# First attention of a two-block fp32 model: forget rows earlier, the head groups' norm and turn earlier, modulation steps partly behind the attention

## The chip, the cores and the metric

The kernel runs on one core of one Trainium2 chip. The metric is the device time of one execution in microseconds. The unchanged kernel took 992.53 us, the median of three runs (992.22, 992.53 and 996.78).

## The reference

The input is one sequence of 256 tokens with 1024 channels in fp32. The first block is: RMS norm, one projection, eight heads of "forgetting" attention and eight heads of "stick-breaking" attention (head width 64), an RMS norm of each group of eight heads, an output projection, a gated feed-forward part with a causal convolution of three taps, and a final RMS norm. The second block has two layers whose norms are modulated by `mod = silu(c) @ w_ada + b_ada`, 6 x 1024 numbers a layer.

```python
F = cumsum(log_sigmoid(f_logit + forget_bias))                    # per head
logits = q.k/sqrt(64) + F[t] - F[s], s <= t; p = softmax(logits); o_fox = p @ v
A[t,s] = sigmoid(z[t,s]) * prod_{s<j<t}(1 - sigmoid(z[t,j])), s < t;  o_sb = A @ v
o = concat(rmsnorm(o_fox, fox_out_g), rmsnorm(o_sb, sb_out_g)); x = x + o @ w_out
h = rmsnorm(x, ffn_norm_g); u = causal_dwconv(h @ w_up); x = x + (silu(gate) * val) @ w_down
mod = silu(c) @ w_ada[i] + b_ada[i]     # two layers, 1024 x 6144 each, used from the second block on
```

## The kernel before

**Weights.** All weights pass through TensorE in chunks of 1 MB, numbered through the kernel: `IN1` 0 to 11 (projection), `OUT1` 12 to 15 (output), `UP1` 16 to 37, `DOWN1` 38 to 48, `QKV` 49 on. A chunk has two units (h = 0, 1), so unit number u = 2c + h. SyncE loads a chunk into one of four raw buffers, as soon as the low part of the chunk four before it has been made. ScalarE rounds a unit to its high part (`split_unit`, L504), VectorE subtracts to get its low part (L856), and TensorE multiplies with both. There are four buffers of high and low parts: ScalarE makes the high part of unit u when TensorE has finished unit u - 4 (`unit_done`). One unit is 24 matmuls (hi x hi, lo x hi, hi x lo).

**Order.** Every engine's program is written out by hand, and an engine does its instructions strictly in that order. In the first attention, all engines walk over slots (c, h), c from 0 to 13: TensorE multiplies unit (c, h), the other two prepare unit (c + 2, h), and tables (`SCORES1`, `EXPS1`, `PROBS1`, `VALUES1`) say in which slot each head's scores, exponentials, turns and value products come. Heads 0 to 7 are the forgetting group (g = 0), 8 to 15 the stick-breaking group (g = 1). `place(c)` on VectorE (L1140 to L1152) takes a projected chunk out of the PSUM bank to its place. The slots in `EARLY` do this ahead of the slot's split.

**Forget rows.** `forget` on ScalarE (L691, L693) and `nlf` on VectorE (L1249) give -log f; `forget_sums` on TensorE (L1697 to L1703) sums it up. VectorE copies the sums (`f_rows`, L1252), ScalarE issues two small DMAs that put them into spare rows of the keys (`forget_move`, L699), and TensorE's first scores (L1712) wait for these, for `f_cum`, and for the first two placed chunks.

**Group norms.** For g = 0: VectorE `fox_outputs` (L1203), ScalarE `output_squares` (L708), VectorE `output_mean` (L1220), ScalarE `output_rms` (L715, L717), VectorE `output_norm` (L1227 to L1232), TensorE `output_turn` (eight transposes, L1788), then ScalarE `output_hi` (L725) and VectorE `output_lo` (L1239). The same for g = 1, whose turned halves are the operand of the second half of the output projection (`out1_chunk(2, ...)` on); the first half, `out1_chunk(0 and 1, ...)`, uses g = 0.

**Modulation.** GpSimd pulls 1 MB pieces of `w_ada` (`fetch`, L458) into two buffers; VectorE adds each to an accumulator (`ada(n)`, L871). The pull for step n is issued when step n - 2 is done. Steps 0 to 7 sit in slots of the first attention (`ADA_AT1`), 8 to 13 in the pairs of `UP1` (`ADA_UP1`), 14 and 15 at the head of `DOWN1`, 16 to 23 in its loop. TensorE's `mod_sums(0)` (L1636) needs steps 0 to 7.

**After the output projection** VectorE's `add_up` splits units 32 and 33, and adds four PSUM banks to the residual (L943); ScalarE squares them (L509), TensorE sums the squares (L1521), then `mod_sums(0)`, and after the norm the first up-projection (L1452). In a pair of `UP1` VectorE splits four units (L856), does its `ada` if it has one, eight convolution steps (L965) and two steps for the hidden rows (L978, L981).

Of the kernel before, what the change touches and what calls it, by code (L numbers as in the profile page):

```python
# [8 lines left out]
ALU = mybir.AluOpType  # L9
# [47 lines left out]
PROBS2 = [(4, 0), (5, 0), (6, 0), (7, 0), (9, 0), (10, 0), (11, 1), (12, 1)]  # L57
VALUES2 = [(5, 0), (6, 0), (8, 0), (8, 1), (11, 0), (11, 1), (12, 1), (13, 1)]

ADA_AT1 = [(3, 0), (4, 0), (4, 1), (5, 0), (6, 0), (7, 0), (7, 1), (8, 0)]  # L60
ADA_UP1 = (1, 3, 4, 6, 8, 9)
ADA_AT2 = [(0, 0), (2, 0), (5, 0), (7, 0), (8, 0), (10, 0), (12, 0), (13, 0)]
LAST = 12
QK_AT, V_AT = (0, 1, 2, 3, 5, 6, 8, 9), (4, 7, 10, 11)
# [24 lines left out]
def model_kernel(nc, x, attn_norm_g, w_in, forget_bias, fox_out_g, sb_out_g, w_out, ffn_norm_g, w_up,  # L89
# [3 lines left out]
    with ctx:  # L93
# [396 lines left out]
        def _(act):  # L490
# [238 lines left out]
            for c in range(14):  # L729
                for h in range(2):  # L730
                    if (c, h) == (1, 0):
                        forget()
                    if (c, h) == (1, 1):
                        act.wait_ge(f_rows_ready, 1)
                        act.wait_ge(pad_set, 4)
                        forget_move()
                    if (c, h) == (13, 0):
                        output_squares(1)
                        output_rms(1)
                    if c < LAST:  # L740
                        split_unit(c + 2, h)
                    attend(c, h)
                    if (c, h) == (2, 1):
                        act.wait_ge(vec_ready, 4)
                        act.activation(silu_e[:], vec[:, 0, V_C:V_C + KT], ACT.Exp, scale=-1.0).then_inc(silu_r, 1)
                    if c >= LAST:
                        split_unit(c + 2, h)
                    if (c, h) == (9, 0):
                        output_squares(0)
                    if (c, h) == (9, 1):  # L750
                        output_rms(0)
                    if (c, h) == (10, 1):
                        output_hi(0)
            act.wait_ge(unit_done, 2 * OUT1)
            output_hi(1)
            split(OUT1 + 4)
            squares(1, 1)
            norm(1, 1, late=(UP1 + 1, 0))
# [85 lines left out]
        def _(dve):  # L844
# [139 lines left out]
            def gated_layer(c0, pair0, straight, convolve, ada0=None):  # L984
                def step(c, pair, p, i, j=None):
                    split(c + 2, i)
                    split(c + 3, i)
                    if ada0 is not None and i is not None:
                        ada(ada0 + j, i)
                    if c0 == UP1 and p in ADA_UP1:  # L990
                        ada(8 + ADA_UP1.index(p))
                    gated_pair(c, pair, p, i, convolve)
                for p in range(straight):
                    step(c0 + 2 * p, pair0 + p, p, None)
                if straight == PAIRS:
                    return
                ada_step[0] = 2
                with dve.Fori(0, (PAIRS - straight) // 2) as i:
                    for j in range(2):
                        p = straight + j  # L1000
                        step(c0 + 2 * p, pair0 + p, p, i, j)
                ada_step[0] = 4

            def down_layer(c0, ada0, gate):
                def rows(d, i=None):
                    if d:
                        split_unit(c0 + d + 1, 1, i)
                    split_unit(c0 + d + 2, 0, i)
                for d in range(2):
                    if c0 == DOWN1:  # L1010
                        ada(14 + d)
                    rows(d)
                if c0 == DOWN3:
                    for k in range(KT):
                        dve.tensor_scalar(gate_diag[:, k, :], ident[:], mod[:, 1, G_F + k:G_F + k + 1], None, ALU.mult
                                          ).then_inc(diag_ready, 1)
                    for d in range(2, 9):
                        rows(d)
                    split_unit(c0 + 10, 1)
                    dve.wait_ge(x_tok_ready, 4)  # L1020
                    dve.wait_ge(gate_ready, 2)
                    for j in range(4):
                        t, g = j // 2, slice(j % 2 * 512, (j % 2 + 1) * 512)
                        if j < 3:
                            dve.wait_ge(bank_done, BANKS_DONE[c0] + j + 1)
                        else:
                            dve.wait_ge(unit_done, 2 * (c0 + 11))
                        dve.tensor_tensor(o_sb[:, t, g], bank[4 + j][:, :], gate_row[:, g], ALU.mult).then_inc(o_scaled, 1)
                        dve.wait_ge(o_scaled, j + 1)
                        dve.tensor_tensor(o_sb[:, t, g], o_sb[:, t, g], x_tok[:, t, g], ALU.add).then_inc(out_ready, 1)  # L1030
                    return
                else:
                    with dve.Fori(0, 2) as i:
                        for j in range(4):
                            ada(ada0 + j, i)
                            rows(2 + j, i)
                    split_unit(c0 + 11, 1)
                for j in range(4):
                    if j < 3:
                        dve.wait_ge(bank_done, BANKS_DONE[c0] + j + 1)  # L1040
                    else:
                        dve.wait_ge(unit_done, 2 * (c0 + 11))
                    update(bank[4 + j], j, gate)
# [58 lines left out]
            link(dve.tensor_scalar(f_neg[:], f_sum[:], -1.0, 0.0, ALU.mult, ALU.max))  # L1102
            dve.wait_ge(x_spread, 1)
            link(dve.tensor_copy(x_scale, bank[SPREAD_BANK][:, 0:T]))
            x_res(2)
            x_res(3)
            split_unit(1, 1)

            def vectors_turned():

# [130 lines left out]
                    ins.then_inc(ot1_lo, 1)  # L1241


            EARLY = ((1, 1), (4, 1), (7, 1), (9, 1), (10, 1), (11, 1))
            for c in range(14):
                for h in range(2):
                    if (c, h) == (0, 0):
                        dve.wait_ge(f_act, 3)
                        dve.tensor_tensor(nlf[:], f_neg[:], f_log[:], ALU.add).then_inc(nlf_ready, 1)  # L1249
                    if (c, h) == (1, 1):  # L1250
                        dve.wait_ge(cum_done, 1)
                        dve.tensor_copy(f_rows, bank[3][0:4, :]).then_inc(f_rows_ready, 1)  # L1252
                        dve.tensor_scalar(f_cum[:], bank[2][:, 16:32].rearrange("p (t n) -> p t n", n=8), -1.0, None,
                                          ALU.mult).then_inc(cum_ready, 1)
                    if (c, h) in EARLY:
                        place(c)
                    if (c, h) == (13, 0):
                        output_mean(1)
                        output_norm(1)
                    if c < LAST:  # L1260
                        split_unit(c + 2, h)
                    if (c, h) == (8, 1):
                        fox_outputs()
                    if (c, h) == (2, 0):
                        vectors_turned()
                    if (c, h) == (3, 0):
                        silu()
                    attend(c, h)
                    if c >= LAST:
                        split_unit(c + 2, h)  # L1270
                    if h == 1 and c < 12 and (c, h) not in EARLY:
                        place(c)
                    if (c, h) == (9, 1):
                        output_mean(0)
                        output_norm(0)
                    if (c, h) == (10, 1):
                        output_lo(0)
                    if (c, h) in ADA_AT1:
                        ada(ADA_AT1.index((c, h)))
            output_lo(1)  # L1280
            add_up(OUT1)
            norm(1, lambda k: vcol(0, V_FFN + k), late=(UP1 + 1, 0))
            split_unit(UP1 + 1, 1)
# [129 lines left out]
        def _(pe):  # L1413
# [70 lines left out]
                for h in range(2):  # L1484
                    half_chunk(c, h, dst, src_hi, src_lo, i, operand)

            def output_chunk(c0, n, h, k_hi, k_lo, ready=None):

# [6 lines left out]
                for outputs in (range(4),) if n < 3 else (range(2), range(2, 4)):  # L1497
                    for r in tiles:
                        k = 4 * (n // 2) + 2 * h + r
                        if ready is not None and outputs[0] == 0:  # L1500
                            ready(k)
                        w_unit = u if r >= 0 else u - 1
                        for o in outputs:
                            w = slice(r % 2 * 2 * CW + o * P, r % 2 * 2 * CW + (o + 1) * P)
# [286 lines left out]
            def out1_chunk(n, h):  # L1791
                if (n, h) == (0, 0):
                    pe.wait_ge(proj_free, 12)
                if (n, h) == (1, 0):
                    pe.wait_ge(t_ready, 8)
                output_chunk(OUT1, n, h, lambda k: (fox_hi if k < 4 else act_hi)[:, k, :],
                             lambda k: (fox_lo if k < 4 else act_lo)[:, k, :],
                             lambda k: pe.wait_ge(ot1_lo, k // 2 + 1))

            for c in range(14):  # L1800
                if 2 <= c < 12:
                    pe.wait_ge(proj_free, c - 1)
                for h in range(2):
# [16 lines left out]
                    attend(c, h)  # L1820
                    if (c, h) == (10, 0):
                        output_turn(0)
            output_turn(1)
            for n in (2, 3):
                for h in range(2):
                    out1_chunk(n, h)
# [125 lines left out]
```

## Time and profile before

| what | value |
|---|---|
| median of three runs | 992.53 us |
| the profiled execution | 996.4 us |
| its span | 994.8 us |
| mean granted TensorE clock | 0.991 |
| TensorE matmuls busy | 966.7 us (97%) |
| VectorE busy | 716.3 us (72%) |
| ScalarE busy | 482.4 us (48%) |
| DMA, mean | 209 GB/s |

The profiled execution spends 1.6 us outside its span. TensorE is busy nearly all the time, so time can be lost in two ways: it stands still, or its clock is granted at half. The stretches below are in us from the start of the span.

### The profile page before, as it was taken

How to read it: one execution, taken by the hardware profiler on the slowest of the kernel's cores; microseconds unless marked ns; L12 is line 12 of the kernel's file. 1: busy time of each engine (PE TensorE's matmuls, PEld its weight loads, DVE VectorE, ACT ScalarE, POOL GpSimd, SP SyncE). 2: the span in 40 equal slices, each digit the busy share in tenths (PEclk: the TensorE clock that was granted, in tenths of full speed). 3: DMA queues.
4: the chain of work that ended last, by engine and by line, in shares of the span. 5: the costliest groups of instructions: out<-in, count | busy, mean ns of one | idle time of the engine just before them, and what ended most of it. 6: DMA issues, size and time to landing. Idle time of an engine off the chain costs nothing.

```text
span 994.8 us, 18807 instructions
## 1 busy us (share of the span) xinstructions
PE 966.7 (97%) x7571; PEld 939.0 (94%) x7571; DVE 716.3 (72%) x942; ACT 482.4 (48%) x704; POOL 45.3 (5%) x79
## 2 busy tenths in 40 slices
PE   8899899999999999999999999999999999999998
PEld 7899889999999989899999999999999999999876
DVE  6699757788898869887775777877766575555544
ACT  5345645565555345554454444434544454444541
POOL 4000000000010100000000001000000000000000
PEclk9899999999999999999999999999999999999999
DMA  9688232666667966566646778796555445555441
GB/s 305 212 279 313 87 128 87 210 211 235 235 240 294 371 231 211 182 207 205 211 141 197 256 263 278 269 368 215 169 171 178 161 132 197 178 172 192 168 144 43
DMA packets 130969, 207.61 MB, mean 209 GB/s; under 512 B 4582, under 2 KB 109408, under 8 KB 124768
## 3 DMA queue, kind: packets, MB, share of 16 engines
q1 hardware_dynamic: 122784, 156.43, 46.8%
q0 software_dynamic: 6912, 50.33, 14.2%
q8 instruction: 40, 0.66, 0.3%
q10 hardware_dynamic: 1216, 0.05, 0.1%
q14 instruction: 17, 0.14, 0.0%
HBM read 205.75 MB, written 1.05 MB: 208 GB/s over the span
## 4 chain that ended last, share of the span: by engine, by line
PE 71%; DVE 18%; issue 4%; DMA 3%; ACT 3%; POOL 0%; ACTq 0%; DVEq 0%; POOLq 0%
PE bank L1416 21%; PE bank L1418 21%; PE bank L1417 21%; DVE w_lo L856 5%; DVE ada_acc L871 4%; DMA ada_raw<-in_w_ada 3%; PE bank L1521 2%; DVE conv L965 1%; ACT w_hi L504 1%; PE bank L1452 1%; PE bank L1457 1%; PE bank L1454 1%; DVE scr L891 1%; PE bank L1636 1%; DMA k_fox<-sb_l 0%
## 5 line engine op out<-in xcount | busy, mean ns | idle before, releaser
L856 DVE TENSOR_TENSOR w_lo<-w_raw,w_hi 128x1024 fp32r<-128x1024 f32 x294 | 354.7, 1223 | 177.5 <-ACT w_hi L504 174.4
L504 ACT ACTIVATE w_hi<-w_raw 128x1024 fp32r<-128x1024 f32 x294 | 305.6, 1054 | 280.1 <-PE bank L1418 270.1
L1416 PE MATMUL bank<-act_hi,w_hi 128*128 128x256 f32 x1440 | 410.5, 285 | 3.1 <-DVE act_lo L1239 2.4
L1417 PE MATMUL bank<-act_lo,w_hi 128*128 128x256 f32 x1440 | 407.4, 283 | 0.0
L1418 PE MATMUL bank<-act_hi,w_lo 128*128 128x256 f32 x1440 | 407.4, 283 | 0.0
L1416 PEld LDWEIGHTS bank<-act_hi,w_hi 128*128 128x128 f32 x1440 | 276.2, 192 | 4.7 <-DVE w_lo L856 4.3
L1417 PEld LDWEIGHTS bank<-act_lo,w_hi 128*128 128x128 f32 x1440 | 276.3, 192 | 0.3 <-issue 0.2
L1418 PEld LDWEIGHTS bank<-act_hi,w_lo 128*128 128x128 f32 x1440 | 276.2, 192 | 0.0
L871 DVE SCALAR_TENSOR_TENSOR ada_acc<-ada_raw,silu_c,ada_acc 128x2048 f32<-128x2048 f32 x48 | 112.6, 2346 | 11.4 <-DMA ada_raw<-in_w_ada 11.4
L1416 PE MATMUL bank<-hid_hi,w_hi 128*128 (+1 forms) x352 | 99.5, 283 | 3.7 <-DVE w_lo L856 3.7
L1418 PE MATMUL bank<-hid_hi,w_lo 128*128 (+1 forms) x352 | 99.1, 281 | 0.0
L1417 PE MATMUL bank<-hid_lo,w_hi 128*128 (+1 forms) x352 | 99.0, 281 | 0.0
L1416 PEld LDWEIGHTS bank<-hid_hi,w_hi 128*128 128x128 f32 x352 | 66.8, 190 | 4.4 <-issue 4.4
L1418 PEld LDWEIGHTS bank<-hid_hi,w_lo 128*128 128x128 f32 x352 | 66.9, 190 | 0.0
L1417 PEld LDWEIGHTS bank<-hid_lo,w_hi 128*128 128x128 f32 x352 | 66.7, 189 | 0.0
L554 ACT ACTIVATE hid_hi<-hidden 128x512 f32 (+1 forms) x33 | 20.9, 632 | 70.4 <-DVE hidden L978 70.4
L458 POOL DMA_DIRECT2D ada_raw<-in_w_ada x48 | 25.5, 532 | 609.9 <-DVE ada_acc L871 594.0
L981 DVE TENSOR_TENSOR hid_lo<-hidden,hid_hi 128x512 f32 (+1 forms) x33 | 22.9, 692 | 28.9 <-ACT hid_hi L554 28.9
L1416 PE MATMUL bank<-w_hi,act_hi 128*128 128x256 f32 x128 | 39.7, 310 | 0.0
L1417 PE MATMUL bank<-w_lo,act_hi 128*128 128x256 f32 x128 | 38.2, 298 | 0.0
L1418 PE MATMUL bank<-w_hi,act_lo 128*128 128x256 f32 x128 | 38.0, 297 | 0.0
L1416 PE MATMUL bank<-ot_hi,w_hi 128*128 128x256 f32 x128 | 36.0, 281 | 0.0
(283 smaller groups left out, 1244.1 us busy)
## 6 DMA issues: line engine op xcount, KB each, us to landing
ada_raw<-in_w_ada POOLq DMA_DIRECT2D x48, 1024.0 KB, 5.5
w_raw<-in_w_gate_up SPq DMA_DIRECT2D x44, 1024.0 KB, 5.1
w_raw<-in_w_down SPq DMA_DIRECT2D x33, 1024.0 KB, 5.0
w_raw<-in_w_in SPq DMA_DIRECT2D x23, 1024.0 KB, 7.2
w_raw<-in_w_up SPq DMA_DIRECT2D x22, 1024.0 KB, 5.3
w_raw<-in_w_qkv SPq DMA_DIRECT2D x12, 1024.0 KB, 7.8
w_raw<-in_w_out SPq DMA_DIRECT2D x8, 1024.0 KB, 5.1
w_raw<-in_w_o SPq DMA_DIRECT2D x4, 1024.0 KB, 5.8
```

Of the source, the lines that this page charges most:

```text
L458: pool.dma_start(ada_raw[:, j, :], w_ada_2[l][cols(j * P, 2 * P, i, P), s * ADA_W:(s + 1) * ADA_W]).then_inc(ada_landed[j], 16)
L504: act.activation(unit(w_hi, u), raw_half(c, h), ACT.Copy).then_inc(hi_ready, 1)
L554: act.activation(hid_hi[:, cols(2 * p, 4, i, 2), :], hidden[:], ACT.Copy).then_inc(hid_hi_r, 1)
L856: dve.tensor_tensor(unit(w_lo, u), raw_half(c, h), unit(w_hi, u).bitcast(F32), ALU.subtract).then_inc(lo_ready, 1)
L871: dve.scalar_tensor_tensor(ada_acc[:, s, :], ada_raw[:, n % 2, :], silu_c[:, cols(k, ada_step[0], i, 1)], ada_acc[:, s, :], ALU.mult, ALU. ...
L891: dve.scalar_tensor_tensor(scr[:, k, :], res[:, k, :], gain(k), rstd[:], ALU.mult, ALU.mult).then_inc(hx_ready, 1)
L965: ins = dve.scalar_tensor_tensor(conv[:, q, lag:T], src[:, (q % 2) * T:(q % 2 + 1) * T - lag], vcol(tile, base + f, 4, i), conv[:, q, lag: ...
L981: dve.tensor_tensor(hid_lo[:, kt, :], hidden[:], hid_hi[:, kt, :].bitcast(F32), ALU.subtract).then_inc(hid_lo_r, 1)
L1416: pe.matmul(dst, a_hi, b_hi, start=start, stop=False, skip_group_check=True)
L1417: pe.matmul(dst, a_hi, b_lo, start=False, stop=False, skip_group_check=True)
L1418: return pe.matmul(dst, a_lo, b_hi, start=False, stop=stop, skip_group_check=True)
L1521: ins = pe.matmul(bank[SUM_BANK[n]][:, 0:T], w, scr[:, k, :], start=k == 0, stop=k == KT - 1)
```

## The change

It has four parts. (1) VectorE computes `nlf` ahead of the last two residual copies and of unit 3, and copies the forget sums in slot (0, 1) instead of (1, 1); chunk 0 is now placed after that. (2) For g = 0 the squares move from slot (9, 0) to (8, 1), the mean and `rms` from (9, 1) to (9, 0), and `output_norm(0)` to the head of (9, 1); TensorE's turn stays where it was. (3) For g = 1 the turn moves between the two halves of unit 27, and `output_hi(1)`, `output_lo(1)` ahead of the split of unit 31. (4) Modulation steps 6 and 7 move from (7, 1) and (8, 0) to (11, 0) and (12, 0); steps 8 to 10 stand between the attention and `add_up`; 11 to 15 in pairs 1, 3, 5, 7, 9 of `UP1`; the head of `DOWN1` has none.

```diff
-ADA_AT1 = [(3, 0), (4, 0), (4, 1), (5, 0), (6, 0), (7, 0), (7, 1), (8, 0)]
-ADA_UP1 = (1, 3, 4, 6, 8, 9)
+ADA_AT1 = [(3, 0), (4, 0), (4, 1), (5, 0), (6, 0), (7, 0), (11, 0), (12, 0)]
+ADA_UP1 = (1, 3, 5, 7, 9)
...
 # ScalarE
+                    if (c, h) == (13, 1):
+                        act.wait_ge(unit_done, 2 * OUT1)
+                        output_hi(1)
                     if c >= LAST:
                         split_unit(c + 2, h)
+                    if (c, h) == (8, 1):
+                        output_squares(0)
                     if (c, h) == (9, 0):
-                        output_squares(0)
-                    if (c, h) == (9, 1):
                         output_rms(0)
...
-            act.wait_ge(unit_done, 2 * OUT1)
-            output_hi(1)
...
 # VectorE
-                        ada(8 + ADA_UP1.index(p))
+                        ada(11 + ADA_UP1.index(p))
...
-                    if c0 == DOWN1:
-                        ada(14 + d)
                     rows(d)
...
+            dve.wait_ge(f_act, 3)
+            dve.tensor_tensor(nlf[:], f_neg[:], f_log[:], ALU.add).then_inc(nlf_ready, 1)
+            split_unit(1, 1)
             x_res(2)
             x_res(3)
-            split_unit(1, 1)
...
-            EARLY = ((1, 1), (4, 1), (7, 1), (9, 1), (10, 1), (11, 1))
+            EARLY = ((0, 1), (1, 1), (4, 1), (7, 1), (9, 1), (10, 1), (11, 1))
-                    if (c, h) == (0, 0):
-                        dve.wait_ge(f_act, 3)
-                        dve.tensor_tensor(nlf[:], f_neg[:], f_log[:], ALU.add).then_inc(nlf_ready, 1)
-                    if (c, h) == (1, 1):
+                    if (c, h) == (0, 1):
                         dve.wait_ge(cum_done, 1)
                         dve.tensor_copy(f_rows, bank[3][0:4, :]).then_inc(f_rows_ready, 1)
...
+                    if (c, h) == (9, 1):
+                        output_norm(0)
...
                     attend(c, h)
+                    if (c, h) == (13, 1):
+                        output_lo(1)
...
-                    if (c, h) == (9, 1):
+                    if (c, h) == (9, 0):
                         output_mean(0)
-                        output_norm(0)
...
-            output_lo(1)
+            for n in range(8, 11):
+                ada(n)
             add_up(OUT1)
...
 # TensorE: output_chunk calls between() ahead of the second half (r == 1) of unit 27
-                             lambda k: pe.wait_ge(ot1_lo, k // 2 + 1))
+                             lambda k: pe.wait_ge(ot1_lo, k // 2 + 1),
+                             (lambda: output_turn(1)) if (n, h) == (1, 1) else None)
...
-            output_turn(1)
```

## Rows read from the trace of the kernel before

**Rows 1.** The page, busy time, share of the span and instructions of each engine.
```profile
PE 966.7 (97%) x7571; PEld 939.0 (94%) x7571; DVE 716.3 (72%) x942; ACT 482.4 (48%) x704; POOL 45.3 (5%) x79
```
**Rows 2.** Waits of TensorE, whole span: us in total, times, longest us.
```profile
PE bank L1416 <- DVE w_lo L856: 4.4, 5, 1.9
...
PE bank L1756 <- DVE fox_lo L1239: 1.5, 1, 1.5
...
PE bank L1697 <- DVE nlf L1249: 0.6, 1, 0.6
```
**Rows 3.** Windows: length, busy us of PE, PEld, DVE, ACT, POOL, clock, DMA share, GB/s.
```profile
34.00:40.00 6.00, 5.96 (x26) 5.81 (x27) 1.72 (x7) 0.00 (x0) 0.00 (x0) 0.50 0.55 176
142.00:144.00 2.00, 0.00 (x0) 0.00 (x0) 2.00 (x4) 1.39 (x4) 0.00 (x0) 1.00 0.01 4
354.00:357.00 3.00, 3.00 (x16) 3.00 (x16) 2.21 (x3) 0.39 (x1) 0.00 (x0) 0.50 1.08 388
```
**Rows 4.** Timeline of VectorE around the forget rows: start us, us.
```profile
20.21 1.29 DVE L1067 COPY res<-bank 128x512 f32<-128x512 f32 x2
21.42 1.21 DVE L856 TENSOR_TENSOR w_lo<-w_raw,w_hi 128x1024 fp32r<-128x1024 f32 x1
22.55 0.17 DVE L1249 TENSOR_TENSOR nlf<-f_neg,f_log 128x16 f32<-128x16 f32 x1
...
24.91 1.39 DVE L1152 SCALAR_TENSOR_TENSOR q_pad<-bank,ada_acc 64x512 f32<-64x512 f32 x2
...
27.58 0.68 DVE L1252 COPY sb_l<-bank 4x512 f32<-4x512 f32 x1
```
**Rows 5.** Timeline of ScalarE, the small DMAs' issue.
```profile
28.29 1.32 ACTq L699 DMA_DIRECT2D k_fox<-sb_l  x2
```
**Rows 6.** Timeline of TensorE, idle before an instruction in brackets.
```profile
34.04 0.77 PE L1712 MATMUL bank<-k_fox,q_pad 128*128 128x128 f32 x2 [2.85 <-DMA k_fox<-sb_l]
...
104.62 2.06 PE L1788 MATMUL bank<-ident,o_tok 128*128 128x128 f32 x8 [2.38 <-DVE o_tok L1232]
...
140.67 1.04 PE L1788 MATMUL bank<-ident,o_tok 128*128 128x128 f32 x8
144.12 0.35 PE L1416 MATMUL bank<-act_hi,w_hi 128*128 128x256 f32 x1 [2.42 <-DVE act_lo L1239]
155.71 3.61 PE L1521 MATMUL bank<-scr,ones 128*128 128x256 f32 x16
159.16 3.73 PE L1636 MATMUL bank<-ones,ada_acc 128*128 128x128 f32 x32
163.52 0.36 PE L1452 MATMUL bank<-act_hi,w_hi 128*128 128x256 f32 x1 [0.63 <-ACT act_hi L531]
353.39 0.36 PE L1416 MATMUL bank<-hid_hi,w_hi 128*128 128x256 f32 x1 [1.91 <-DVE w_lo L856]
```
**Rows 7.** Timeline of VectorE: a modulation step, the two norms, the last update.
```profile
84.45 2.35 DVE L871 SCALAR_TENSOR_TENSOR ada_acc<-ada_raw,silu_c,ada_acc 128x2048 f32<-128x2048 f32 x1
...
102.74 0.16 DVE L1220 TENSOR_SCALAR small<-small 128x2 f32<-128x2 f32 x1
...
137.73 1.41 DVE L1232 TENSOR_SCALAR o_tok<-bank,small 128x512 f32<-128x512 f32 x2
...
155.91 0.69 DVE L943 TENSOR_TENSOR res<-bank,res 128x512 f32<-128x512 f32 x1 [1.17 <-PE bank L1418]
```
**Rows 8.** Timeline of GpSimd: the pull of step 9.
```profile
91.90 0.53 POOL L458 DMA_DIRECT2D ada_raw<-in_w_ada  x1 [3.91 <-DVE ada_acc L871]
```
**Rows 9.** DMA issues: KB each, median us to landing.
```profile
out<-ada_acc SPq DMA_DIRECT2D x4, 256.0 KB, 2.1
...
f_bias<-in_forget_bias ACTq DMA_DIRECT2D x1, 4.0 KB, 7.7
```
**Rows 10.** All pulls of modulation weights, from issue to landing.
```profile
DMA to landing us min/median/max: 5.0/5.5/9.7
```
**Rows 11.** Chain of waits in DOWN1: start us, us, what.
```profile
318.36 8.35 DMA ada_raw<-in_w_ada
```

More of the change, by code:

```diff
@@ L1485, in chunk, with output_chunk @@
                     half_chunk(c, h, dst, src_hi, src_lo, i, operand)
-            def output_chunk(c0, n, h, k_hi, k_lo, ready=None):
+            def output_chunk(c0, n, h, k_hi, k_lo, ready=None, between=None):
                 u = 2 * (c0 + n) + h
@@ L1501, in output_chunk @@
                             ready(k)
+                        if between is not None and r == 1:
+                            between()
                         w_unit = u if r >= 0 else u - 1
```

## The prediction

> **What bounds the kernel now.** I read the page first: TensorE's matmuls are busy for 966.7 of 994.8 us, VectorE for 716.3 [rows 1]. No other engine is full over the whole span, so time can go only where TensorE stands still or its clock is low. The list of TensorE's waits comes second: the reader is to see single stalls, none of them large, at the forget sums (0.6), the forget rows, the turn, `fox_lo` (1.5), the second turn, and five times 4.4 us in all at a weight's low part [rows 2]; the places and lengths stand in the timeline [rows 6]. Third come the windows: behind three of these stalls (34 to 40, 105 to 108, 354 to 357) the granted clock is 0.50, that is 1.2 instead of 2.4 GHz, and behind another one, of 2.42 us, it is 1.00 [rows 3, 6]. A stall thus costs its length and sometimes the half clock behind it. The engines' timelines come last, for what each stall waits for. Between 50 and 100 us VectorE is idle for under 2%, but its low parts are ready some 8 us before TensorE takes them, so it paces nothing there.
>
> **Term 1, forget rows: 5.8 us gained.** Today two residual copies (1.29) and unit 3's split (1.21) stand ahead of `nlf`, which starts at 22.55 [rows 4]. After the change it follows the scale copy at about 20.3. TensorE, through with unit 2 at 22.17, no longer waits 0.60 for it [rows 2], and the sums end at 24.4 instead of 25.0. VectorE meanwhile does unit 3's split, the two residual copies and unit 4's split (1.2 + 1.3 + 1.2) from 20.4 to 24.1, waits for the sums, and starts the copy of the rows at 24.5, not 27.58: 3.1 us earlier. The two small DMAs follow at once; from their issue at 28.29 to the scores at 34.04 it is 5.75 us [rows 5, 6]. With the same transit the scores start at 24.45 + 0.7 + 5.75 = 30.9, against 34.04: 3.1 us. TensorE would get there at 31.19 - 0.60 = 30.6, so 0.3 us of stall stays. Is something else late then? The scores also need chunk 1 placed. That is the copy of rows and sums (0.7), chunk 0's place (1.4), two splits (2.4) and chunk 1's place (1.4 [rows 4]): 24.5 + 5.9 = 30.4, just in time. Unit 5, now split behind chunk 0's place, is ready at 27.7 and used at 31.6. SyncE is moved by it: the load that waits for unit 5 is issued 2.7 us later, but its chunk is rounded only some 15 us after that. With 0.3 us of stall I expect no half clock. From 34.04 on, scores, 24 matmuls and scores took 6.7 us at half clock; the same three at full clock, one unit later, are 4.0. So 2.7 more, 5.8 in all.
>
> The transit is the uncertain size: the trace's small or unhindered transfers lie between 2.1 us (the output) and 7.7 us (the forget bias, under load) [rows 9], and the two windows compared are both full of weight traffic. At 2.1 the gain is 6.1, since TensorE itself isn't there earlier; at 7.7 the scores start 2 to 2.8 us later and the half clock stays: 0.5 gained. I take the present 5.75, same pair of DMAs under the same load. (The Trainium skill, "DMA: Bandwidth & Descriptors", section "Queues, rings and completion order", says that each DMA engine takes turns between the queues that have work, a packet at a time. By that rule the megabytes queued by SyncE wouldn't lengthen the small DMAs' way, and the term would be the same at any load; no row here separates the two.)
>
> **Term 2, first turn: 3.7 us gained.** In present times less the shift of term 1: dropping modulation steps 6 and 7 (2.26 us each, start to start [rows 7]) lets VectorE do `fox_outputs` at 90.7 to 92.2 instead of 92.3 to 93.8. ScalarE squares right behind it (1.2), which makes unit 22's high part end at 94.4 instead of 93.1; no one needs that before 106. The mean ends at 97.7 instead of 102.9 [rows 7], `rms` at 98.2, and the norm, behind place(9) and unit 23's split, at 101.8. TensorE is free for the turn at 102.1: the stall of 2.38 [rows 6] goes, by a margin of 0.3 us. The half clock behind it made transposes and 24 matmuls 5.5 us long, 3.9 at full rate (1.0 for the eight transposes at 140.67 [rows 6]): 1.6. What is late next is `fox_lo`, at which TensorE waits 1.5 us today [rows 2]: the norm now stands ahead of the stick-breaking work of (9, 1) and pushes it, so that `output_lo(0)` ends some 6.25 us behind unit 21 instead of 5.95. That gives back 0.3. 2.4 + 1.6 - 0.3 = 3.7. Bounds: 0 (both stalls as long as before, merely moved) and 4.3.
>
> **Term 3, second turn and steps 6 to 10: 5.8 us lost.** Still in present times for the attention's end. Step 6 in (11, 0) delays place(11) to 124.6, just before TensorE's 124.85: free. Step 7 in (12, 0) takes 2.26 us in a stretch where VectorE has about 0.95 us idle, so `output_norm(1)`, now ending at 139.14 (137.73 + 1.41 [rows 7]), ends at 140.4. TensorE, half through unit 27, comes to the turn at 139.3 and waits 1.2. Then turn and second half (2.4) end at 142.8, when the first pair of low parts is there too: 144.12 [rows 6] becomes 142.85, 1.27 gained of the 2.42.
>
> Unit 27 now ends at 143.1, so unit 31's split is over at 145.4. Then come steps 8, 9, 10. The pulls of 8 and 9 have long landed: a pull goes out 0.7 us behind the step two before it (91.90, after step 7's end at 91.2 [rows 8]). The pull of 10 goes out 0.7 us behind step 8, at 148.3, and takes 5.0 to 9.7, median 5.5 [rows 10]: 154.0. VectorE has nothing to do from 149.9 on. Step 10 ends at 156.3, units 32 and 33 are split by 158.6, four updates at 0.84 us end at 161.8, where the last one ended at 156.6 [rows 7]. TensorE has finished the output projection at 154.6 and stands for about 5 us. The squares' sums end at 163.4 instead of 159.2, unit 34's split, hidden today by the sums, stands ahead of the norm for another 0.6, and the first up-projection starts at 163.5 + 4.8 = 168.3 [rows 6]. After so long a pause I expect the half clock, as after the 2.85 us one. It runs mostly in the pause; `mod_sums(0)` (3.7 at full rate [rows 6]) has 0.6 us to spare, and I charge 1.0. Sum: -5.8. Ends: -4.3 (landing in 5.0, no half clock) and -11.5 (landing in 9.7, 3.4 us of half-clock matmuls on the path).
>
> (The Trainium skill, "TensorE: Matmul & The Clock Gate", section "Loop structure matters more than you think", warns against waits between bursts of matmuls, since the clock drops over them. It speaks against this term. The rows agree in part: 2.85 us were followed by 0.50, 2.42 us by 1.00.)
>
> **Term 4, UP1 and DOWN1: 6.1 us gained.** A pair costs TensorE 11.7 us, VectorE 10.2, or 12.5 with a step. Today pairs 3, 4 and 8, 9 have steps in a row, and the stalls behind them are 0.73 (at 234.08) and 0.81 (at 293.25). Alternating pairs catch up, so both go. The head of DOWN1 has two steps, and stalls of 0.63 and 0.31 behind them; both go. In DOWN1's loop each odd step waits for a pull that waits for the step before it; one such wait is 8.35 us [rows 11], a round 11.5, and three rounds from step 17 (315.36) to step 23 (349.76) end in the stall of 1.91 at 353.39 [rows 6]. Steps 16 and 17 now find their data landed and VectorE 4.6 us earlier: step 17 at 310, step 23 at 344.6, its split by 348.1, used at 350.3. The stall goes. 0.73 + 0.81 + 0.63 + 0.31 + 1.91 = 4.4, the five times of [rows 2]. The half clock of 354 to 357.6 [rows 3] held 1.7. Bounds 3.0 (the last round late by 2 as before, with no half clock) and 6.1.
>
> **Sum.** 5.8 + 3.7 - 5.8 + 6.1 = 9.8 us off the profiled execution's 996.4 us: 986.6. That execution is 3.9 us above the median, near the slowest of the three runs; the trace can't say why the two others are quicker. Half-clock stretches that they lack would be a cause, and then these can't be gained again. 992.5 - 9.8 = 982.7; for a third of the 3.9 being such I add 1.3: **984.0 us**.
>
> **Rivals.**
> - *The pause before UP1 is heavier* (0.12). Same mechanism as term 3 at its far end, -11.5: 15.6 - 11.5 = 4.1 gained, about 989.5. For it: the pull meets a chunk's load, as in DOWN1 with 8.35 [rows 11]. Against it: the median of 5.5.
> - *The small DMAs stay late* (0.08). Term 1 gives 0.5: 4.5 gained, about 989. For it: the 7.7 of [rows 9]. Against: nothing about these DMAs changes but the time.
> - *VectorE takes term 1 back* (0.09). It is full from 50 to 100; if its 8 us of lead shrink by the 5.8 that TensorE gains, the next small delay shows: 4.0 gained, 989.8. Against: its own idle time at 37 to 41.6 waits for TensorE and moves along.
> - *Term 3 is free* (0.09), if the wait for step 10 falls beside something I have missed: 978.
> - *Slower* (0.06): the three steps behind the attention each wait for their own pull. Place: ahead of `add_up`. A round as in DOWN1 is 11.5, three are 34.5 where I count 10.9 from 145.4 to 156.3, so the loss is 5.8 + 23.6 = 29.4 against 15.6 of gains: 1006. It decides from 15.6 us of loss on. Against it: the pulls of 8 and 9 depend on steps 6 and 7, 20 and 7 us earlier [rows 8].
>
> **How the numbers follow.** The forecast has 0.56, its own range is 979.5 to 987.5. The range of 978 to 990 holds it and the neighbours, and leaves out the slower case and the tails. What a measurement can tell from no change is about 0.5%, 5 us, so the border is 987.6. Faster: nearly all of the forecast (0.54), the free case (0.09), and a third of the three near cases (0.09): 0.72. Slower: 0.06. Same: 0.22.
>
> **What would show it.** Right: the wait for the forget rows under 1 us, clock 1.00 between 31 and 37; no wait at the first turn; about 1 us at the second; VectorE waiting some 4 us for a pull just after the attention and TensorE idle about 5 us ahead of the squares' sums; no wait for a low part in UP1 and DOWN1. Wrong: low clock moved to another stretch, a wait for the rows above 2 us, or no gap ahead of the sums.

## The result: 0.8% faster, against 0.9% forecast

The changed kernel takes 986.26 us (median of 9 executions, 985.68 to 989.0). The kernel before, run beside it, takes 994.06 us (median of 9, 991.0 to 998.46). The ratio is 0.9924, 95% interval 0.9903 to 0.9944. The forecast was 984.0 us against 992.5, a ratio of 0.991.

| | before | after |
|---|---|---|
| profiled execution, us | 996.4 | 985.69 |
| its span, us | 994.8 | 984.1 |
| mean granted clock | 0.991 | 0.998 |
| matmuls busy, us | 966.7 | 961.3 |

The page's busy times of after answer to [rows 1]. Work and instructions are the same; the 5.4 us fewer of TensorE go with less half clock (a mean of 0.998 instead of 0.991).

```profile
PE 961.3 (98%) x7571; PEld 933.4 (95%) x7571; DVE 716.6 (73%) x942; ACT 482.1 (49%) x704; POOL 45.3 (5%) x79
```

TensorE's waits from 15 to 170 us of after, in us in total, times, longest, answer to [rows 2]. The line numbers of this kernel are 1 to 4 higher than before.

```profile
PE bank L1525 <- ACT scr L509: 4.5, 1, 4.5
PE bank L1760 <- DVE fox_lo L1240: 1.9, 1, 1.9
PE bank L1792 <- DVE o_tok L1233: 0.7, 2, 0.4
PE bank L1454 <- ACT act_hi L531: 0.6, 1, 0.6
PE bank L1716 <- DMA k_fox<-sb_l: 0.4, 1, 0.4
```

The wait for `nlf` is gone, that for the forget rows is 0.4 instead of 2.85, the first turn has 0 instead of 2.4, the second has 0.7 and the wait of 2.4 for the low part behind it is gone, and a new wait of 4.5 stands ahead of the squares' sums. The whole span holds no wait for a weight's low part any more (five before). The same places in TensorE's timeline, answering to [rows 6]:

```profile
31.34 0.46 PE L1716 MATMUL bank<-k_fox,q_pad 128*128 128x128 f32 x2 [0.41 <-DMA k_fox<-sb_l]
...
96.72 1.04 PE L1792 MATMUL bank<-ident,o_tok 128*128 128x128 f32 x8
...
106.94 0.41 PE L1760 MATMUL bank<-v_tok,sb_b 128*128 128x64 f32 x2 [1.93 <-DVE fox_lo L1240]
...
149.89 5.41 PE L1525 MATMUL bank<-scr,ones 128*128 128x256 f32 x16 [4.48 <-ACT scr L509]
155.14 3.73 PE L1640 MATMUL bank<-ones,ada_acc 128*128 128x128 f32 x32
159.50 0.36 PE L1454 MATMUL bank<-act_hi,w_hi 128*128 128x256 f32 x1 [0.62 <-ACT act_hi L531]
```

VectorE's timeline of after, against [rows 4] and [rows 7]: `nlf` (L1105) right behind the scale copy, the rows' copy (L1250) at 24.78 instead of 27.58, and behind the attention three modulation steps, the third starting after 3.30 us of waiting for its data.

```profile
20.77 0.17 DVE L1105 TENSOR_TENSOR nlf<-f_neg,f_log 128x16 f32<-128x16 f32 x1 [0.18 <-ACT f_log L693]
...
24.78 0.68 DVE L1250 COPY sb_l<-bank 4x512 f32<-4x512 f32 x1 [0.37 <-PE bank L1707]
...
135.79 4.80 DVE L872 SCALAR_TENSOR_TENSOR ada_acc<-ada_raw,silu_c,ada_acc 128x2048 f32<-128x2048 f32 x2
143.89 2.35 DVE L872 SCALAR_TENSOR_TENSOR ada_acc<-ada_raw,silu_c,ada_acc 128x2048 f32<-128x2048 f32 x1 [3.30 <-DMA ada_raw<-in_w_ada]
...
150.95 0.69 DVE L944 TENSOR_TENSOR res<-bank,res 128x512 f32<-128x512 f32 x1 [0.15 <-DVE res L944]
```

GpSimd issues the pull of step 10, the late one, 0.7 us behind step 8. It lands 5.1 us later; the rule of [rows 8] holds again.

```profile
138.80 0.53 POOL L458 DMA_DIRECT2D ada_raw<-in_w_ada  x1 [10.26 <-DVE ada_acc L872]
```

The windows of after (columns as in [rows 3]): full clock behind the forget rows and from 290 to 360 us (the end of UP1 and most of DOWN1), half clock only behind the new pause.

```profile
31.00:37.00 6.00, 5.66 (x44) 5.59 (x45) 4.90 (x11) 2.91 (x7) 0.00 (x0) 1.00 1.08 343
...
150.00:154.00 4.00, 4.00 (x11) 3.24 (x12) 2.04 (x3) 2.84 (x4) 0.00 (x0) 0.57 0.97 339
...
290.00:360.00 70.00, 69.87 (x568) 68.85 (x568) 56.33 (x57) 33.41 (x45) 6.05 (x9) 1.00 0.82 300
```

### The profile page after: what moved, and what is told of

Same layout as the page of the kernel before. It is cut to its first block, busy times and chain, and to the rows that moved or that the text cites. A ratio compares the mean times of both kernels' runs of the same rounds, so it can differ in the third digit from the quotient of the medians.

```text
span 984.1 us, 18808 instructions
## 1 busy us (share of the span) xinstructions
PE 961.3 (98%) x7571; PEld 933.4 (95%) x7571; DVE 716.6 (73%) x942; ACT 482.1 (49%) x704; POOL 45.3 (5%) x79
## 4 chain that ended last, share of the span: by engine, by line
PE 81%; DVE 12%; ACT 3%; issue 2%; DMA 1%; POOL 0%; ACTq 0%; DVEq 0%; POOLq 0%
PE bank L1418 24%; PE bank L1419 24%; PE bank L1420 24%; DVE w_lo L857 3%; DVE ada_acc L872 2%; PE bank L1525 2%; PE bank L1454 1%; PE bank L1459 1%; ACT w_hi L504 1%; PE bank L1456 1%; DVE scr L892 1%; PE bank L1640 1%; DMA ada_raw<-in_w_ada 1%; DMA k_fox<-sb_l 1%; ACT act_hi L535 0%
## 5 line engine op out<-in xcount | busy, mean ns | idle before, releaser
L1418 PE MATMUL bank<-w_hi,act_hi 128*128 128x256 f32 x128 | 37.4, 292 | 0.0
L1419 PE MATMUL bank<-w_lo,act_hi 128*128 128x256 f32 x128 | 36.2, 283 | 0.0
```

The lines of the kernel that those rows point to most:

```text
L1418: pe.matmul(dst, a_hi, b_hi, start=start, stop=False, skip_group_check=True)
L1419: pe.matmul(dst, a_hi, b_lo, start=False, stop=False, skip_group_check=True)
```

## A ruler for the experiments

Every profile was cut at five starts of TensorE: the first product, the first forget scores, the value products of head 8 (the place of the `fox_lo` wait), the first up-projection, and the first head sums in the second block. So A is term 1's waits, B the first attention with the first turn, C the rest of the attention with the second turn and the output projection, D UP1 and DOWN1. What lies ahead of A varies by itself: the first product starts at 9.71 to 11.31 us in the thirteen profiles. What lies behind D takes 607.8 to 608.15 us in all of them. Times in us; "half clock in" names the sections in which windows show a clock near 0.5.

| kernel | A | B | C | D | half clock in |
|---|---|---|---|---|---|
| before | 24.32 | 82.20 | 47.28 | 223.25 | B twice, D |
| after | 21.20 | 75.60 | 52.56 | 216.78 | C |
| p1_rows | 21.18 | 79.54 | 47.27 | 221.36 | B |
| p2_norm | 24.43 | 78.81 | 51.88 | 220.56 | B, C twice |
| p2_norm_steps | 24.38 | 78.27 | 47.28 | 221.24 | B |
| p4_steps | 24.38 | 80.97 | 52.31 | 216.82 | B twice, C |
| fill_rows | 24.14 | 79.65 | 47.30 | 221.08 | B |
| after_fill | 21.31 | 75.60 | 52.89 | 216.79 | C |
| step10_later | 21.27 | 75.61 | 46.11 | 218.20 | none |
| turn_back | 21.22 | 75.61 | 56.68 | 216.82 | C twice |
| pair0_1 | 21.24 | 75.61 | 46.12 | 217.68 | none |
| lo_early | 21.26 | 73.75 | 46.12 | 217.66 | none |
| after_again | 21.26 | 75.61 | 55.11 | 216.79 | C twice |

## The experiments

**Each part alone, on the kernel before.** First the forget rows:

```diff
+            dve.wait_ge(f_act, 3)
+            dve.tensor_tensor(nlf[:], f_neg[:], f_log[:], ALU.add).then_inc(nlf_ready, 1)
+            split_unit(1, 1)
             x_res(2)
             x_res(3)
-            split_unit(1, 1)
...
-            EARLY = ((1, 1), (4, 1), (7, 1), (9, 1), (10, 1), (11, 1))
+            EARLY = ((0, 1), (1, 1), (4, 1), (7, 1), (9, 1), (10, 1), (11, 1))
...
-                    if (c, h) == (1, 1):
+                    if (c, h) == (0, 1):
                         dve.wait_ge(cum_done, 1)
```

> The kernel before with part 1 alone (nlf, forget sums' copy and chunk 0's place earlier). Theory of term 1: TensorE waits 0.3 to 0.5 us for the forget rows instead of 2.85, none for nlf, and the clock is 1.00 from 31 to 37; everything up to the first turn comes 5.8 us earlier and stays so, since VectorE's own idle time moves along: 5 to 6.5 us faster by the profile. Rival (VectorE takes it back): new waits for low parts between 50 and 100 us, and less than 2 us are left at the end.

Measured: 989.77 us, ratio 0.9949 (0.9927 to 0.997). Its timeline:

```profile
31.62 0.46 PE L1711 MATMUL bank<-k_fox,q_pad 128*128 128x128 f32 x2 [0.40 <-DMA k_fox<-sb_l]
...
99.57 2.06 PE L1787 MATMUL bank<-ident,o_tok 128*128 128x128 f32 x8 [2.40 <-DVE o_tok L1234]
```

A is 3.14 us shorter and C is unchanged. B is 2.66 shorter, although its own waits are the same as before: that is the half clock that no longer follows the rows. A and B together give the 5.8 us of term 1; the medians are 5.0 apart. No new wait arises in B, and the waits for low parts in D add up to 4.4 us as before, so VectorE takes nothing back; that rival falls.

Then the first group's norm (squares at (8, 1), rms and mean at (9, 0), the norm ahead of attend(9, 1)), without and with the move of steps 6 and 7; the list of steps is changed in `p2_norm_steps` only:

```diff
+                    if (c, h) == (8, 1):
+                        output_squares(0)
                     if (c, h) == (9, 0):
-                        output_squares(0)
-                    if (c, h) == (9, 1):
                         output_rms(0)
...
+                    if (c, h) == (9, 1):
+                        output_norm(0)
...
-ADA_AT1 = [..., (7, 0), (7, 1), (8, 0)]
+ADA_AT1 = [..., (7, 0), (11, 0), (12, 0)]
```

> The kernel before with the first group's squares, mean, rms and norm moved, modulation steps 6 and 7 left in (7, 1) and (8, 0). Theory: the steps' 4.5 us stand ahead of fox_outputs, so the norm ends at about 103.6 and TensorE still waits about 1.5 us at the turn (2.38 before): under 1 us gained, 2.5 if the half clock behind it goes too. Rival: the norm's place alone is enough, no wait at the turn and 3.7 us gained.

> The same with modulation steps 6 and 7 moved to (11, 0) and (12, 0). Theory of term 2: no wait at the first turn, clock 1.00 behind it, fox_lo waited for 1.9 instead of 1.5 us: 3.7 to 4.0 us earlier at that point. Step 7 then delays the second norm by 1.3 us, but with the turn at its old place behind unit 27 that is just hidden. In all 3.5 to 4 us faster.

Measured: `p2_norm` 993.8 us, ratio 0.9986 (0.9967 to 1.0004); `p2_norm_steps` 991.48 us, ratio 0.9964 (0.9944 to 0.9984). The first keeps a wait of 0.67 at the turn and gets 2.24 at `fox_lo`:

```profile
103.06 1.29 PE L1789 MATMUL bank<-ident,o_tok 128*128 128x128 f32 x8 [0.67 <-DVE o_tok L1232]
113.85 0.57 PE L1757 MATMUL bank<-v_tok,sb_b 128*128 128x64 f32 x2 [2.24 <-DVE fox_lo L1239]
```

The second has no wait at the turn and 1.94 here:

```profile
112.36 0.41 PE L1757 MATMUL bank<-v_tok,sb_b 128*128 128x64 f32 x2 [1.94 <-DVE fox_lo L1239]
```

So the norm's place takes 1.7 us of the turn's 2.4 (I had expected 1.5 us of wait to stay), but 0.7 of that comes back at `fox_lo`; moving the two steps takes the last 0.67 and 0.3. Waits alone: 2.4 + 1.55 before, 0.67 + 2.24, and 0 + 1.94 here, that is 1.0 and 2.0 us gained, half of it by the norm's place. The times of `p2_norm` can't be told from before; those of `p2_norm_steps` are 3.3 us lower, 3.5 to 4 having been expected. The step moved to (12, 0) costs nothing with the turn at its old place: C is 47.28, to the hundredth as before.

Then the modulation steps alone:

```diff
-ADA_UP1 = (1, 3, 4, 6, 8, 9)
+ADA_UP1 = (1, 3, 5, 7, 9)
...
+            for n in range(8, 11):
+                ada(n)
             add_up(OUT1)
```

> The kernel before with modulation steps 8 to 10 behind the attention, 11 to 15 in pairs 1, 3, 5, 7, 9, none at the head of DOWN1; nothing else. Theory: VectorE waits 3 to 4 us for step 10's pull, the first up-projection starts 4.5 to 5.5 us later behind the output projection; UP1 and DOWN1 have no wait for a low part and are 6 to 6.5 us shorter: 0.5 to 2 us faster in all, even if the half clock of 354 to 357 goes. Rival: the gap is hidden by the squares' sums, then 6 us faster.

Measured: 993.12 us, ratio 0.9992 (0.9973 to 1.0011), no difference that can be told; the medians are 1.7 us apart. C grows by 5.03, D shrinks by 6.43 against the kernel before, or by 3.7 to 4.5 against the profiles that have the old steps and no half clock in D (220.56 to 221.36). VectorE waits for the pull, and TensorE then for the squares:

```profile
152.77 2.35 DVE L871 SCALAR_TENSOR_TENSOR ada_acc<-ada_raw,silu_c,ada_acc 128x2048 f32<-128x2048 f32 x1 [3.48 <-DMA ada_raw<-in_w_ada]
```
```profile
158.77 5.41 PE L1521 MATMUL bank<-scr,ones 128*128 128x256 f32 x16 [3.07 <-ACT scr L509]
```

**What the half clock is worth.** TensorE was given work, of no use, during the wait for the forget rows of the kernel before, and during the new pause of the changed kernel. The first addition is that of `fill_rows`, the second that of `after_fill`:

```diff
+                        idle_turns(11, 1)
                         pe.wait_ge(f_moved, 32)
...
+            idle_turns(18, 5)
             square_sums(1)
```

> The kernel before with eleven idle 128-column products of ones in a spare bank ahead of the wait for the forget rows: TensorE works through most of the 2.85 us wait instead of standing. Theory: the scores start at 34.0 as before, but the clock stays 1.00 behind them, and the 2.7 us that I put down to the half clock come back: 2.5 to 2.9 us faster. Rival: the clock falls for another reason (the short matmuls before it, or its own time), then no gain and 0.50 again from 34 to 40.

> The changed kernel with eighteen such idle products ahead of the squares' sums behind the output projection. Theory: they fill the pause of 4.5 us, the squares' sums run at full clock (5.41 us for them becomes about 3.7) and 0.5 to 1.5 us come back. Rival: the sums are paced by the squares, not by TensorE, and nothing is gained.

Measured: `fill_rows` 993.05 us, ratio 0.9992 (0.9974 to 1.0011). Its profile does what was expected: the scores start as late as ever, the clock behind them is 1.00, and B is 2.55 us shorter.

```profile
35.12 0.49 PE L1712 MATMUL bank<-k_fox,q_pad 128*128 128x128 f32 x2 [0.18 <-DMA k_fox<-sb_l]
```
```profile
35.00:41.00 6.00, 5.88 (x46) 5.78 (x47) 2.97 (x9) 2.04 (x6) 0.00 (x0) 1.00 0.49 165
```

But over twelve executions no gain can be told from the noise, and the lower end of the interval, 0.9974, is a gain of 2.6 us: the 2.5 to 2.9 that I had expected in every execution are at its edge or outside. One profile agrees with the mechanism at this place; the times don't confirm its size. `after_fill` takes 985.72 us, ratio 0.9918 (0.9891 to 0.9944). The squares' sums run at full clock:

```profile
152.20 3.72 PE L1525 MATMUL bank<-scr,ones 128*128 128x256 f32 x16 [0.64 <-ACT scr L509]
```

C is no shorter (52.89): in this execution half clock followed the `fox_lo` wait instead. The median is 0.5 us below the changed kernel's in its own runs and 1.9 below in `after_again`, but neither ran beside it, and the intervals of the three ratios overlap: a gain is not shown.

**Step 10 behind the norm.**

```diff
-ADA_UP1 = (1, 3, 5, 7, 9)
+ADA_UP1 = (0, 2, 4, 6, 8, 10)
...
-            for n in range(8, 11):
+            for n in range(8, 10):
```

> The changed kernel with steps 8 and 9 alone behind the attention and 10 to 15 in pairs 0, 2, 4, 6, 8, 10 of UP1. Theory of term 3: the wait for step 10's pull (3.3 us) and the step (2.3) leave the path ahead of the squares, TensorE's pause of 4.5 us goes and the half clock with it: 5 to 6.5 us faster than the changed kernel, and UP1 and DOWN1 hold no wait. Rival: the pair without slack brings a wait for a low part in UP1, and under 3 us are left.

Measured: 981.93 us, ratio 0.9888 (0.986 to 0.9916), 4.3 us below the changed kernel in its own runs (5 to 6.5 had been expected). C is 46.11, 6.45 less than in the changed kernel and 1.17 less than before the change: that is term 3's gain at the second turn, laid bare (1.27 forecast). The step in pair 10 costs a wait in DOWN1, which I had not expected, and D is 1.42 us longer than in the changed kernel:

```profile
294.89 0.38 PE L1418 MATMUL bank<-hid_hi,w_hi 128*128 x1 [1.73 <-DVE w_lo L857]
```

**The second turn back at its old place.**

```diff
-                             (lambda: output_turn(1)) if (n, h) == (1, 1) else None)
+                             None)
...
+            output_turn(1)
             for n in (2, 3):
```

> The changed kernel with the second turn back behind unit 27; output_hi(1) and output_lo(1) stay ahead of unit 31's split. Theory: the turn no longer waits 0.7 us, but TensorE stands 1.3 to 2 us for the first low part instead, so the output projection ends 0.9 to 1.5 us later; the pause behind it takes that up, since VectorE, not TensorE, ends it: under 0.5 us of difference at the end. Rival: the whole 1.2 us show at the end.

Measured: 987.49 us, ratio 0.9937 (0.9914 to 0.996). The wait at the low part is 1.55 and the pause is as long as in the changed kernel. C reads 56.68, but its windows show half clock twice; clean profiles of both kernels would be needed to separate the rest. The times (987.49 against 986.26 and 987.57) show no clear difference, which fits the expectation that the pause takes the loss up.

```profile
137.67 0.35 PE L1418 MATMUL bank<-act_hi,w_hi 128*128 128x256 f32 x1 [1.55 <-DVE act_lo L1240]
...
153.89 2.50 PE L1525 MATMUL bank<-scr,ones 128*128 128x256 f32 x5 [4.47 <-ACT scr L509]
```

The medians of parts 1, 2 and 4 were 5.0, 3.3 and 1.7 us lower, 10.0 in all against 7.8 for the whole change. Each is known to about 2 us, so the difference can't be told from noise.

**Better than both.** Two further kernels, and the changed kernel again beside them. Both have the new steps; `lo_early` alone has the other two additions, on ScalarE and on VectorE:

```diff
-ADA_UP1 = (1, 3, 5, 7, 9)
+ADA_UP1 = (0, 1, 3, 5, 7, 9)
...
-            for n in range(8, 11):
+            for n in range(8, 10):
...
+                    if (c, h) == (10, 1):
+                        output_hi(0)
                     attend(c, h)
...
+                    if (c, h) == (10, 1):
+                        output_lo(0)
```

> The changed kernel with steps 8 and 9 alone behind the attention and 10 to 15 in pairs 0, 1, 3, 5, 7, 9 of UP1 (0, 2, 4, 6, 8, 10 in the run before this one, which left a wait of 1.73 us at a low part in DOWN1 behind pair 10). Theory: VectorE sits idle 3 us for high parts in pair 0, so the steps of 0 and 1 may follow each other, and no step stands right ahead of DOWN1: no wait for a low part at all, 1.3 to 1.8 us faster than that kernel, about 980. Rival: the two steps in a row bring 0.7 us of wait in UP1 as pairs 3 and 4 did in the kernel before, then about 981.

> The same, and the first group's output_hi and output_lo ahead of the stick-breaking work of slot (10, 1) on ScalarE and VectorE instead of behind it. Theory: the low halves of the first group are ready some 1.7 us earlier, and TensorE's wait of 1.93 us ahead of the value products falls to 0.3 or less: 1.5 to 2 us faster than without, about 978.5. Rival: the stick-breaking steps, now 1.7 us later, hold TensorE in slot (11, 0) or (11, 1) instead, and nothing is gained.

> The changed kernel itself, as the common neighbour of the two others on the same chip. It should lie 0.7 to 0.9% below the kernel before, and its executions should spread by 3 to 4 us with the mean granted clock, 0.994 to 0.998.

Measured: `pair0_1` 981.75 us, ratio 0.9879 (0.9854 to 0.9905). The rival was right: a wait of 0.74 follows the two steps in a row, instead of 1.73 behind pair 10, and the time is that of `step10_later`.

```profile
189.93 0.39 PE L1418 MATMUL bank<-act_hi,w_hi 128*128 128x256 f32 x1 [0.74 <-DVE w_lo L857]
```

`after_again` takes 987.57 us, ratio 0.9931 (0.9906 to 0.9956), `lo_early` 978.46 us, ratio 0.9843 (0.9819 to 0.9867): B is 1.86 shorter and the wait for `fox_lo` is gone from the list.

```profile
105.00 0.41 PE L1760 MATMUL bank<-v_tok,sb_b 128*128 128x64 f32 x2
```
```profile
core 0: 976.6 us, clock 1.000
```

Its six executions lie within 1.0 us (978.04 to 979.01) at clocks of 0.999 and 1.000, where `pair0_1`, with the one wait of 1.94 more, spreads over 3.2 us at 0.996 to 0.999. The medians are 3.3 us apart, more than the wait. Of the 3.2 us between the two profiles, which hold no half clock in A to D, 1.86 are B and 1.32 are the start of the first product, 11.31 against 9.99 us, which the edits don't touch.

## Why the prediction was right, step by step

**Term 1, waits: 3.1 forecast, 3.1 measured.** A went from 24.32 to 21.20. The scores wait 0.41 (0.3 forecast), on a transit from issue to scores of 5.84 us against 5.75 [rows 5, 6]. That the low or high end of [rows 9] would hold instead is ruled out here. No run varied the load on the queues, so whether the small DMAs' way depends on it stays open.

**Term 2, waits: 2.1 forecast (2.4 less 0.3), 2.0 measured.** No wait at the turn, 1.93 at `fox_lo` against 1.85 forecast. In the experiments half of the gain came with the norm's place and half with the moved steps.

**Term 3: 5.8 lost forecast, 5.3 measured.** C went from 47.28 to 52.56, of which about 1.3 is half clock (1.0 forecast; the estimate stands below). Of its steps, the turn's wait was 0.7 instead of 1.2, the pull took 5.1 instead of 5.5, and the pause was 4.5 instead of 5. The cause is shown by `step10_later`: with step 10 taken out of the place, C falls to 46.11. The slower rival (three pulls one after another) is out: steps 8 and 9 run back to back.

**Term 4, waits: 4.4 forecast, 3.8 to 4.6 measured** (D is 220.56, 221.08, 221.24 and 221.36 in the four profiles with the old steps and no half clock there, and 216.78 after). The pieces differ from profile to profile: `p1_rows` has 0.73, 0.83, 1.04, 0.32, 0.39 and 1.08, with the same sum as before. Step 23, which ends the last round of DOWN1, starts 179.5 us behind the first up-projection where it was 186.2, 6.7 us less (5.2 forecast).

```profile
339.01 2.35 DVE L872 SCALAR_TENSOR_TENSOR ada_acc<-ada_raw,silu_c,ada_acc 128x2048 f32<-128x2048 f32 x1 [0.46 <-DMA ada_raw<-in_w_ada]
```

**Half clock: 5.0 us forecast (2.7 + 1.6 + 1.7 - 1.0), mis-sized as a fixed sum.** In the profile of before it stood at the three places that I had named, and at a fourth that I had missed, in the second block, about 2 us behind a wait of 1.11:

```profile
427.08 1.05 PE L1848 MATMUL bank<-ones,h_sq 128*128 128x1 f32 x8 [1.11 <-ACT q L779]
```
```profile
429.00:433.00 4.00, 4.00 (x23) 4.00 (x23) 4.00 (x4) 0.86 (x4) 0.00 (x0) 0.57 0.50 134
```

In the pair of profiles the named ones had nearly the forecast size: beyond its waits B became shorter by 4.6 us (4.3 forecast) and D by 2.1 (1.7), while C became longer by 1.3 (1.0). The window of 142 to 144 in [rows 3] is the wait of 2.42 us itself; behind it the clock was 1.00 too, as I had written:

```profile
144.00:148.00 4.00, 3.88 (x32) 3.91 (x33) 0.76 (x2) 0.67 (x1) 0.00 (x0) 1.00 0.81 262
```

The stretch in the second block came in 5 of 13 profiles (before, p2_norm, p2_norm_steps, fill_rows, step10_later), with the same wait of 1.11 in all thirteen. It cost only about 0.3 us, since a wait of 1.0 behind it then fell away (behind D, 608.02 to 608.15 us with it and 607.79 to 607.85 without).

The forecast took half clock to come behind the named waits each time. But the same wait is followed by half clock in one execution and not in another. Behind the rows' wait of 2.9 us it came in 4 of 4 profiles (before, p2_norm, p2_norm_steps, p4_steps); behind the first turn's wait of 2.4 in 4 of 4 (before, p1_rows, p4_steps, fill_rows); behind the second group's 2.4 (the low part) in 1 of 6; behind the `fox_lo` wait of 1.94 in 3 of the 7 profiles that have it (after_fill, turn_back, after_again); in D behind the 1.91 of before, but behind none of the other waits there, the longest 1.73. Here are `after_again`, then the changed kernel, behind the same wait:

```profile
109.00:113.00 4.00, 4.00 (x20) 3.79 (x19) 1.44 (x4) 2.33 (x5) 0.00 (x0) 0.57 0.00 0
```
```profile
108.00:112.00 4.00, 4.00 (x33) 3.90 (x32) 1.48 (x4) 2.22 (x5) 0.00 (x0) 1.00 0.02 4
```

Even the first two don't come in every execution: one with a mean clock of 0.998 holds about 5 us of half clock at most (an estimate: twice 0.0025 of 993 us), and the stretches behind the rows and the first turn held some 10 us in the profile of before and some 7 in that of `p4_steps`, the least of all that have both. So at least one of the two was missing in those executions.

The times follow it. Of 65 executions of the kernel before in the experiments, the 13 with a mean granted clock up to 0.9915 have a median of 997.6 us, the 11 at 0.998 and above one of 990.9. A straight line through each kernel's executions gives, at a clock of 1.000, 990.2 us for before and 984.7 for the changed kernel (15 executions): 5.5 us of difference without half clock. The line is no exact tool: its slope is 836 us for a whole unit of clock in one kernel and 655 in the other, and with 836 for both the difference is 6.2. The cuts give 3.1 + 2.0 - 4.0 + 4.4 = 5.5 us of waits (C being 51.2 to 51.3 without its half clock, estimated from `after_fill`, 52.89, less the 1.7 that one half-clock stretch held in D of before). Of the other 2.3 us of the medians' 7.8, about 1.5 are half clock that comes less often: the mean clock is 0.9948 before and 0.9963 after, and 0.0015 of 990 us is 1.5. The last 0.8 is not accounted for.

The profiled execution fell by 10.7 us (9.8 forecast) and the median by 7.8 (8.5 forecast), so taking 1.3 us off for the quicker executions of before was right in kind and about half of the 2.9 that it needed. That the profiles came so near the 9.8 is partly luck: before's was among its slower executions and after's (985.69) among the quickest of nine; with the profile of `after_again`, 988.68, the fall would be 7.7. The median's 8.5 was also helped by errors that cancel: waits of 4.8 us forecast (3.1 + 2.1 - 4.8 + 4.4) where 5.5 were measured, and half clock of 3.7 (5.0 - 1.3) where the clock accounts for about 1.5.

The pauses of 3.07 to 4.7 us ahead of the squares (p4_steps, after, turn_back, after_again) went with a clock near 0.5, from within the pause or just behind it, in 4 of 4 profiles, and filling that pause kept 1.00 in the one profile of it. The Trainium skill's warning of idle gaps ("TensorE: Matmul & The Clock Gate", section "Loop structure matters more than you think") is borne out in direction; the traces add half clock behind waits of 1.94 to 2.9 us as well, and in the second block 1 to 2 us behind one of 1.11, in some executions and not in others.

## What to carry to other kernels

Add up TensorE's waits alone for the sure part of what a change is worth, and count the half clock behind a wait as a chance, not as a part of every execution; one profile shows one draw. Where a producer's data come through two buffers, a third step in a row can wait for its pull, 3.3 to 3.6 us here: put two behind one another, not three, ahead of updates that TensorE waits for. Here the kernel without a wait over 1.11 us behind its start repeated within 0.1%, the one with a single wait of 1.94 within 0.3% (six executions each), and the kernel before within 1.1% (65 executions).

## What was not expected of the hardware

The spread between executions: 989.4 to 1000.2 us for one kernel, most of it the granted clock (correlation of time and mean clock -0.93 over 65 executions), and 978.04 to 979.01 once no wait in the first attention was longer than 0.8 us. Another part is the start, since the first product came at 9.71 to 11.31 us in the profiles for no reason that the edits give; no run shows what moves it.
